# Sparse layer's norms by column sums and a selection moved ahead; the first section with late loads

## The reference

```python
# start of the first block
mod = silu(c) @ w_ada + b_ada                    # six parts; the first two make shift and scale
h = rms_norm(x, g_mix) * (1 + scale) + shift
proj = h @ w_in                                  # latents q_lat (256), kv_lat (128), k_rope (32), ...

# sparse layer, the parts up to its attention
proj = rmsnorm(x) @ w_in                         # c_q (256), c_kv (128), k_idx (64), w_idx (8)
c_q, c_kv, k_idx = rmsnorm(c_q), rmsnorm(c_kv), rmsnorm(k_idx)
q_idx = einsum(c_q, w_q_idx)                     # 8 heads of 64
rel = relu(einsum('bqhd,bsd->bqhs', q_idx, k_idx))
score = einsum('bqh,bqhs->bqs', w_idx, rel)      # masked where the key is later than the query
sel = top_k(score, 128)                          # per query; attention goes over these keys alone
p = masked_softmax(q_abs . c_kv + bias)          # 8 heads
o = p . c_kv
```

## Time and profile before

| | |
|---|---|
| time of the kernel before, median of 3 runs | 2147.43 us (2146.58 to 2153.29) |
| the profiled execution's own time | 2157.64 us, span 2155.7 us |
| TensorE busy | 2009.7 us, 93% of the span |
| VectorE, ScalarE, GpSimd busy | 1005.3, 633.1, 156.7 us |
| granted TensorE clock, mean | 0.96 of full speed |

### The profile page before, as it was taken

How to read it: one execution, slowest core, us unless ns; L and a number is a source line. 1 busy time by engine, 2 the same in 40 slices (tenths; PEclk the granted TensorE clock), 3 DMA queues, 4 the chain that set the end, 5 groups by cost and what they waited for, 6 DMA issues and landing times.

```text
span 2155.7 us, 23513 instructions
## 1 busy us (share of the span) xinstructions
PE 2009.7 (93%) x8895; PEld 1347.8 (63%) x8895; DVE 1005.3 (47%) x1870; ACT 633.1 (29%) x1194; POOL 156.7 (7%) x169
## 2 busy tenths in 40 slices
PE   6989889995999996987999999999899999999998
PEld 3457666673333333535678888875555877888886
DVE  5255544334212115579465545552114757545554
ACT  3373621232111112244442222220024634222222
POOL 1000000020111112103010000020000001000001
PEclk9999999997999997897999999999998999999999
DMA  8323324355999776110122323231431012323211
GB/s 300 132 103 114 121 78 156 119 205 218 408 394 356 290 299 247 52 40 1 48 109 79 117 79 116 79 107 50 153 126 40 1 40 78 115 81 109 86 39 40
DMA packets 103605, 287.06 MB, mean 133 GB/s; under 512 B 13514, under 2 KB 24472, under 8 KB 90448
## 3 DMA queue, kind: packets, MB, share of 16 engines
q1 hardware_dynamic: 91360, 266.24, 33.3%
q0 software_dynamic: 10112, 16.81, 2.2%
q10 hardware_dynamic: 2032, 2.65, 0.4%
HBM read 329.64 MB, written 21.02 MB: 163 GB/s over the span
## 4 chain that ended last, share of the span: by engine, by line
PE 85%; DVE 6%; ACT 2%; DMA 2%; issue 2%; POOL 1%; ACTq 1%; SPq 0%; DVEq 0%; POOLq 0%
PE bank L1282 15%; PE bank L1284 14%; PE bank L1283 14%; PE bank L1199 12%; PE bank L1664 8%; PE bank L1690 4%; PE bank L1241 3%; PE bank L1253 2%; PE bank L1267 2%; PE bank L1850 1%; PE bank L1648 1%; PE bank L1485 1%; PE bank L1273 1%; POOL chunk_mask L1062 1%; DMA weight_ring<-in_w_ada 1%
## 5 line engine op out<-in xcount | busy, mean ns | idle before, releaser
L1284 PE MATMUL bank<-hidden_high,weights_low 128*128 128x512 f32 x896 | 352.1, 393 | 0.0
L1282 PE MATMUL bank<-hidden_high,weights_high 128*128 128x512 f32 x704 | 277.3, 394 | 11.5 <-DVE weights_low L2584 5.0
L2976 DVE TENSOR_TENSOR weights_low<-weight_ring,weights_high 128x1024 fp32r<-128x1024 f32 x128 | 161.1, 1259 | 269.2 <-ACT weights_high L2120 269.2
L1283 PE MATMUL bank<-hidden_low,weights_high 128*128 128x512 f32 x640 | 250.0, 391 | 0.0
L2120 ACT ACTIVATE weights_high<-weight_ring 128x1024 fp32r<-128x1024 f32 x128 | 135.7, 1060 | 323.5 <-PE bank L1284 323.5
L1282 PE MATMUL bank<-normed_high,weights_high 128*128 128x512 f32 x512 | 200.8, 392 | 4.1 <-DVE weights_low L2976 4.0
L1283 PE MATMUL bank<-normed_low,weights_high 128*128 128x512 f32 x512 | 199.9, 390 | 0.0
L1284 PE MATMUL bank<-normed_high,weights_low 128*128 128x512 f32 x512 | 199.8, 390 | 0.0
L1284 PEld LDWEIGHTS bank<-hidden_high,weights_low 128*128 128x128 f32 x896 | 170.4, 190 | 36.2
L1664 PE MATMUL bank<-weight_ring,arena 128*64 128x512 f32 x464 | 174.1, 605 | 4.5 <-issue 2.7
L1199 PE MATMUL bank<-arena,weight_ring 128*128 128x512 f32 x396 | 176.5, 601 | 0.0
(11 more groups left out here) (479 smaller groups left out, 3115.2 us busy)
## 6 DMA issues: line engine op xcount, KB each, us to landing
weight_ring<-in_w_up SPq DMA_DIRECT2D x16, 2048.0 KB, 8.4
weight_ring<-in_w_down SPq DMA_DIRECT2D x16, 2048.0 KB, 7.6
weight_ring<-in_w_gate SPq DMA_DIRECT2D x29, 1024.0 KB
weight_ring<-in_w_up SPq DMA_DIRECT2D x29, 1024.0 KB
weight_ring<-in_w_ada SPq DMA_DIRECT2D x12, 2048.0 KB, 12.7
weight_ring<-in_w_down SPq DMA_DIRECT2D x19, 1024.0 KB
hT<-in_w_down SPq DMA_DIRECT2D x19, 1024.0 KB
weight_ring<-in_w_in SPq DMA_DIRECT2D x7, 2048.0 KB, 12.6
```

The costliest lines, as they stand in the source:

```text
L1282: pe.matmul(dst, high, rhs_high, start=first, stop=False)
L1283: pe.matmul(dst, high, rhs_low, start=False, stop=False)
L1284: return pe.matmul(dst, low, rhs_high, start=False, stop=last)
L2976: dve.tensor_tensor(piece_half(w_lo, ch, q), piece_of(ch, q), piece_half(w_hi, ch, q).bitcast(F32), ALU.subtract).then_inc(s_wlo, 1)
```

## The change

It has these parts:

1. *First section.* 24 of ScalarE's 31 small loads move to SP: the vectors behind the first two `w_ada` chunks, the positions, rotation tables and router biases behind a new empty chunk (`"none"`) that waits for the ring's first slot. The latents' weights leave the ring for the arena, so all four `w_ada` chunks have a slot at once. x's squares are summed token-major by VectorE; root and reciprocal are of 128x4; the reciprocals are put on diagonals and spread by one matmul with ones. `MOD_PE` becomes 4, 4, 0, 0. The angles and sines move behind the first modulation. ScalarE's copies of the value tiles go to VectorE.
2. *Sparse projections.* The latents are scored without their roots. The squares of x and of the latents are summed by matmuls with 32 columns in four column groups side by side, then folded to a column per token and norm. Roots and reciprocals are of 128x20. The key's root comes back as a row (`k_row`), the query's as a column (`q_scale`), both applied when block's scores are copied. The latents for the attention and x itself are scaled later by spread rows; x in steps 19 to 26 of the attention. The index weights are summed in column groups too.
3. *Order.* The scores of block 3 come right behind those of block 2, ahead of `dq`; nine of block 3's sixteen rounds stand ahead of the attention, the other seven at every second step from step 0.
4. *Attention.* The probabilities are normalised by ScalarE instead of VectorE.
5. *GpSimd.* `add_squares(1)` is gone, so the bias table's load is issued right behind the last scatter; GpSimd makes two of the four diagonals.

```diff
-MOD_PE = (4, 3, 2, 2)
+MOD_PE = (4, 4, 0, 0)
+TOP_EARLY = 9
+X_NORMED_FROM = 19
...
     for c in MOD_FIRST:
         chunk(("ada", c), last=G[("mod_sum", c)])
-        if c == MOD_FIRST[1]:
-            chunk("in_lat", last=G["kr"])
+    chunk("none", 0, last=0)
...
                 put_ada(c)
                 if c == MOD_FIRST[1]:
-                    put("in_lat", [(0, kt(w_in, 0, 416))])
+                    load_vectors()
+                    sp.dma_start(w_lat, kt(w_in, 0, 416)).then_inc(s_latw, 16)
+            put("none", [])
+            sp.dma_start(sbuf_s[:, 0, :].bitcast(I32), bass.AP(a["positions"].tensor, 0, [[0, P], [1, T]]))\
...
+            for t in range(NT):
+                dve.wait_ge(s_x[t], 16)
+                junk = hT[:, 2 * t:2 * t + 2, :].rearrange("p a b -> p (a b)")
+                ins = dve.tensor_tensor_reduce(out=junk, in0=x_tok[:, t, :], in1=x_tok[:, t, :], scale=1.0, scalar=0.0,
+                                               op0=ALU.mult, op1=ALU.add, accum_out=x_root[:, t:t + 1])
...
-            add_squares(1)
             pool.wait_ge(mm_done, done(G[("moe_D", STEPS - 1)] + 1))
             pool.dma_start(toe[:, :, :], toe2_dram.rearrange("h p u -> p h u")).then_inc(s_toe, 16)
...
+            for half in range(2):
+                for c in range(4):
+                    last = pe.matmul(psum(g)[32 * c:32 * c + 32, :], w[:, 4 * half + c, 488:520],
+                                     hT[:, 4 * half + c, :], start=(half == 0), stop=(half == 1),
+                                     skip_group_check=True)
...
+            for j in range(KD):
+                pe.wait_ge(s_dxsq, j + 1)
+                pe.matmul(psum(g)[32 * (j % 4):32 * (j % 4) + 32, :], stat_sel[:, j, :], dx_sq[:, j, :], start=(j < 4),
+                          stop=False, skip_group_check=True)
...
             index_scores(1)
+            for n in range(2):
+                pe.wait_ge(s_ddiag, n + 1)
+                token_row(G["token_rows"] + n, n)
             index_scores(2)
+            for n in range(2):
+                pe.wait_ge(s_ddiag_p, n + 1)
+                token_row(G["token_rows_late"] + n, 2 + n)
+            index_scores(3)
+            pe.wait_ge(s_dn, 3)
...
+                    if 0 <= s - 1 < ITEMS:
+                        i = s - 1
+                        h, qt, n = dsa_shape(i)
+                        act.wait_ge(s_rcp, i + 1)
+                        act.activation(sbuf_p[:, i % 3, 0:n], sbuf_p[:, i % 3, 0:n], ACT.Copy,
+                                       scale=stat[:, i % 3, 2:3]).then_inc(s_norm, 1)
...
-                        dve.tensor_scalar(sbuf_p[:, i % 3, 0:n], sbuf_p[:, i % 3, 0:n], stat[:, i % 3, 2:3], None,
-                                          ALU.mult).then_inc(s_norm, 1)
...
+            g_read(dve, G["token_rows"])
             top_rounds(1, 0, TOPK // 8)
+            g_read(dve, G["token_rows"] + 1)
+            for m in range(2):
+                dve.tensor_tensor(cq_n[:, m, :], cq_n[:, m, :], cq_row, ALU.mult).then_inc(s_dn, 1)
+            g_read(dve, G["token_rows_late"])
+            dve.tensor_tensor(ckv_n[:, 0, :], ckv_n[:, 0, :], ckv_row, ALU.mult).then_inc(s_dn, 1)
             top_rounds(2, 0, TOPK // 8)
+            top_rounds(3, 0, TOP_EARLY)
...
-                if s < TOPK // 8:
-                    top_rounds(3, s, s + 1)
+                if s % 2 == 0 and TOP_EARLY + s // 2 < TOPK // 8:
+                    top_rounds(3, TOP_EARLY + s // 2, TOP_EARLY + s // 2 + 1)
+                if s == X_NORMED_FROM:
+                    g_read(dve, G["token_rows_late"] + 1)
+                if X_NORMED_FROM <= s < X_NORMED_FROM + KD:
+                    x_normed(s - X_NORMED_FROM)
```

More of the change, by code:

```diff
@@ L1454, in _, with bias_and_vectors @@
                         last.then_inc(mm_done, 1)
[L1455 to L1465, removed]
+            first_bias_table()
+            g = G["norm_mix"]
+            pe.wait_ge(s_xdiag, 1)
+            tile(g, psum(g)[:, :], [(ones[:, :], x_diag)]).then_inc(mm_done, 1)
+            def bias_and_vectors():
+                first_bias_reversed()
+                pe.wait_ge(s_vec, 16 * 13)
+                g = G["vec"]
+                pe.transpose(begin(g)[:, 0:VN], vec_in[0:VN, :], ident[0:VN, 0:VN]).then_inc(mm_done, 1)
             pe.wait_ge(s_cs, 1)
-            mod_row_sum(MOD_FIRST[0], 0, norm_mix)
+            mod_row_sum(MOD_FIRST[0], 0, bias_and_vectors)
             mod_row_sum(MOD_FIRST[1], 1)
@@ L2165, in _ @@
                            scale=CA_SCALE).then_inc(s_a, 1)
+            for j in range(1, KD, 2):
+                evac(G["tp_x"] + j, xT[:, j, :])
+            g = G["table_T"]
+            evac(g, table1_T[:, :], psum(g)[:, 0:3 * H])
             g = G["toe1"]
@@ L2221, in _ @@
             for m in range(3):
+                if m == 1:
+                    rope_tables()
                 act.wait_ge(mm_done, done(g + m))
@@ L2236, in _ @@
                 evac(g, k_mla[64:128, 2 * p + 1, :], psum(g)[64:128, :])
-            for t in range(NT):
-                evac(G["uv"] + t, v_mla[:, t, :])
             act.wait_ge(s_rv, 16)
@@ new lines, in _ @@
+            dve.wait_ge(s_xroot, 1)
+            link(dve.reciprocal(x_root[:, :], x_root[:, :]))
+            dve.wait_ge(mm_done, done(G["toe2"] + 1))
+            dve.tensor_tensor(x_diag.rearrange("p (t q) -> p t q", t=NT),
+                              ident[:, :].unsqueeze(1).broadcast_to([P, NT, P]),
+                              x_root[:, :].unsqueeze(2).broadcast_to([P, NT, P]), ALU.mult).then_inc(s_xdiag, 1)
+            for j in range(0, KD, 2):
+                evac(G["tp_x"] + j, xT[:, j, :])
@@ new lines, in _, with over_root, first_modulation @@
+            dve.wait_ge(s_cs, 1)
+            mod_partial(MOD_FIRST[0], 0, MOD_PE[0], KD)
+            def over_root(j0, j1):
+                for j in range(j0, j1):
+                    g_read(dve, G["tp_x"] + j)
+                    ins = dve.tensor_tensor(hT[:, j, :], xT[:, j, :], psum(G["norm_mix"])[:, :], ALU.mult)
+                    ins.then_inc(s_unit if j < KD - 1 else freed[G["norm_mix"] % BANKS], 1)
+            def first_modulation(half):
+                for c in MOD_FIRST[2 * half:2 * half + 2]:
+                    mod_add(c)
+                    g_read(dve, G[("mod", c)])
+                scale_of(scale1, 1, "g_mix", half).then_inc(s_mod1, 1)
@@ new lines, in _ @@
+            dve.wait_ge(mm_done, done(G["norm_mix"]))
+            over_root(0, 4)
+            g = G["vec"]
+            evac(g, vecT[:, 0:VN], psum(g)[:, 0:VN])
+            g_read(dve, g)
+            dve.tensor_tensor(gain_sq[:, :], g_first[:, :], g_first[:, :], ALU.mult).then_inc(s_gain, 1)
+            dve.tensor_tensor(gain_both[:, :], g_first[:, :], col("g_attn_2", 0, KD), ALU.mult).then_inc(s_gain, 1)
+            dve.wait_ge(s_gain, 2)
+            mod_partial(MOD_FIRST[1], 1, MOD_PE[1], KD)
@@ L2726, in _ @@
                     .then_inc(freed[g % BANKS], 1)
+            for t in range(NT):
+                evac(G["uv"] + t, v_mla[:, t, :])
             pair_attention("mla")
```

432 lines of the change are left out of this document (200 added, 232 removed).

## The result

The changed kernel takes 2129.74 us (median of 4, 2126.02 to 2132.34) against 2149.31 (4, 2146.58 to 2153.29) beside it: a ratio of 0.9906, 95% interval 0.9881 to 0.9931, or 19.6 us less. The forecast was 41.9 less. A few executions on record took far longer than their neighbours (2163, 3332, 7080 and 11072 us); the ratios leave them out.

The account below looks back on a forecast made before the run. TensorE holds 85% of the chain of waits, while VectorE paces attention steps 0 to 15. The terms -14.4 + 3.1 - 14.0 - 16.6 = -41.9, off the median 2147.43, give 2105.5 us, range 2093 to 2122.

Parts of the forecast that it names:

- the term of 14.0 for projections and selection: Sparse layer, first projection to VectorE's first attention score: 108.1 us against 122.1 now, 14.0 less.
- the first scores last 9.1 as now: Sparse layer, block 1's scores behind the projections: they keep their length of 9.1 us.
- What follows is the same up to the experts' end: From first attention through the experts: unchanged, so the first section's 14.4 us earlier start is kept whole.
- the 0 behind the attention: Stretch from the output weights to the end: the forecast sum has no term for it.
- First section: Start to first attention: latents' halves at 34.8 and 52.8 us, attention starting 14.4 earlier.
- rivals 1 and 4: Late small vector loads: 1 loses half the first section's gain, 2113, chance 0.13; 4 serves them singly, 2171, chance 0.03.
- The hand-over's 3.1: Experts to sparse layer: the bias table's 2 MB load, now behind the last scatter, adds 3.1 us to the path.
- The two groups of tiny matmuls were priced at 1.8: Sparse projections: these matmuls take 1.8 us, an unseen shape, with bounds 0.5 to 4.
- VectorE's chain: Sparse layer, selection rounds of blocks 1 to 3 with latents by their rows: 56.2 us in sum.
- Attention: Attention loop: steps 0 to 15 take 24.5 us against 39.1, 14.6 less; steps 16 to 31 2 less net.
- Rival 2: TensorE stays at 1.2 GHz through attention steps 8 to 15, steps 0 to 15 take 29, table load costs 6: 2113, chance 0.15.
- the 1.5 to 2 set down for that: Attention steps 19 to 26: VectorE's eight scalings of x collide with GpSimd's additions, 1.5 to 2 us lost.

## Why the prediction was wrong, by its own steps

The direction came true, and half of the gain: 18.8 to 20.9 us of 41.9. The step that failed is the term of 14.0 for projections and selection, which measured about 2 to 3; in it "the first scores last 9.1 as now" is what broke. "What follows is the same up to the experts' end" and the 0 behind the attention failed too, by smaller amounts.

The stretches, in us, both profiles of each kernel; the change is between their means:

```
stretch                              before          after          change   forecast
start to first attention             110.5, 110.1    97.2, 96.7     -13.4    -14.4
first attention to first projection  728.0, 722.8    734.7, 734.6   + 9.3    + 3.1
first projection to attention score  122.1, 117.6    118.0, 117.2   - 2.3    -14.0
attention score to output weights     89.7,  88.9     73.1,  73.9   -15.8    -16.6
from there to the end               1105.4, 1105.5  1107.6, 1109.9  + 3.3      0
```

**First section: right.** Latents at 34.55 and 53.78 (forecast 34.8, 52.8), first attention at 97.15 (96.1). The 1 us missing is there when the second half starts. That half then takes 13.52 us for the same 24 matmuls that took 12.07, at the lower clock for part of it, yet from its start to the first attention it is 43.4 us, as forecast (43.3). The vectors were turned at 25.29 (needed at 26), so rivals 1 and 4 are out.

**"What follows is the same up to the experts' end": wrong by some 4 us.** The hand-over's 3.1 is right (3.3 in the trace, 4 when removed). The rest is given back in mixer and experts: from the first attention to the last scatter it is 705.4 and 701.4 us in the two profiles of before, and 705.0 to 710.1, 707.9 on average, in the ten of versions with the new first section, whatever their sparse part. Part of it shows: VectorE waits longer for a block's modulation weights, 6.83 against 5.42 in the first profile of before, and TensorE then waits 1.51 where it had none:

```profile
180.78 0.49 DVE L2639 TENSOR_SCALAR arena<-weight_ring,silu_c 128x512 f32<-128x512 f32 x1 [6.83 <-DMA weight_ring<-in_w_ada]
```

The load is issued 13.3 us earlier, as all else, and lands 9.1 us later instead of 7.7 (8.2 in the second profile of before). The second run of the changed kernel has 6.78 for this wait. Why the load lands later is open; the stretch differs by 5.2 between two executions of one kernel, so its exact share can't be read. The first section alone is worth 11.2 by its times, so by them 2.2 of the 13.4 are given back.

**Projections and selection: the step that failed.** The prediction's sum for the changed kernel was 108.1; it took 118.0. "The first scores last 9.1 as now": they lasted 15.5, since the clock fell, and with VectorE's start behind them this is 7.4 of the 9.9 (18.1 from first score to VectorE's first operation, against 10.7). The two groups of tiny matmuls were priced at 1.8 and took that; what was left out is what they do to the clock of narrow work behind them. Another 1.3 is in the projections (42.5 against 41.2) and 1.2 in VectorE's chain (57.4 against 56.2). The experiments show the cause: a wide query between gives 53.6 instead of 59.8 to 60.6 from first projection to VectorE's start. The other side of this term was one draw: the way of before took 122.1, 117.6 and, in the kernel with the first section alone, 122.2 us. The two long ones are of executions above their kernels' medians (2157.64 over 2147.43, 2148.32 over 2140.97), the short one of an execution below its own (2146.82 under 2151.83). So part of the 14.0, up to 4.5 us, may not have been there to win in a median execution.

**Attention: right.** 23.1 for steps 0 to 15 (forecast 24.5), 1.2 less behind them (forecast 2). The forecast's 39.1 for before is the length of two windows, which begin 0.6 ahead of the first score; from score to score it is 38.6. Rival 2, TensorE at 1.2 GHz through steps 8 to 15, did not come. The scalings of x took 0.73 each (one 0.77), so VectorE lost nothing to GpSimd's additions there; the 1.5 to 2 set down for that did not come there.

**Behind the attention: 1 to 5 lost, forecast 0.** The stretch takes 1105.4 and 1105.5 us before and 1105.5 with the first section alone. Of the nine profiles with the new sparse layer five have 1106.3 to 1106.7, the changed kernel 1107.6, and three 1109.9 to 1110.2; these three have a mean clock of 0.91 from 1500 to 1700 us where the others have 0.94 or 0.95, and one of them is the changed kernel itself, so no edit explains it. One us is a wait: TensorE waits longer for the compression's weights, before and after (line, releaser, us in total, times, longest):

```profile
PE bank L1869 <- DMA weight_ring<-in_cmp_w_v: 0.7, 1, 0.7
```

```profile
PE bank L1933 <- DMA weight_ring<-in_cmp_w_v: 1.8, 1, 1.8
```

**The base.** The terms were read from an execution 10.2 us above the median and taken off the median whole. Part of that excess was in the terms, as the ways of 122.1 and 117.6 show; and the neighbouring series of the kernel before had medians of 2149.3 to 2152.9, not 2147.4.

## What to carry to other kernels

Short matmuls can cost more than their own time: here 1.8 us of them, with narrow matmuls right behind, brought 6 to 7 us at the lower clock. Read the granted clock behind such groups, and try one wide group of independent work between. Here this costs nothing, and gave 6 to 7 us of 2130 in the traces; in the kernel before, where the tiny group itself lasts 9.99 us, wide work behind it came too late. A term that is a difference of two long stretches needs two profiles of before: between them the same stretch moved by 4.5 us, a third of the gain forecast for it. And when an engine starts a loop late because it works ahead for it, look at how much of the work fits in that loop's idle time.

## What the runs showed of the hardware

TensorE's clock can fall with no idle time in its records. In the kernel before it falls inside the 64 matmuls of 8 columns, in a window where TensorE is busy 12.00 of 12.00 us (876 to 888, mean clock 0.75). In the changed kernel it falls about 3 us behind the first tiny matmul, with 0.13 us idle at 875.5; the orders with a query between have the same 0.13 us and no fall. What in these stretches brings the clock down no run shows.

The collision of VectorE and GpSimd falls on the one that starts second. At 977.02 the scaling of x starts, two SBUF inputs, and takes 0.73; GpSimd's addition starts at 977.11 and takes 1.50 where it took 1.01 alone. All eight scalings are like this: GpSimd's four additions of 384 beside them take 1.50 or 1.51, the four of 512 take 1.72 to 1.78 instead of 1.27.

```profile
974.94 1.01 POOL L1208 TENSOR_TENSOR small<-toeplitz_bias,arena 128x384 f32<-128x384 f32 x1 [0.32 <-DVE stat L2552]
977.11 1.50 POOL L1208 TENSOR_TENSOR rtmp<-toeplitz_bias,arena 128x384 f32<-128x384 f32 x1 [1.16 <-DVE stat L2552]
```

The other way round, GpSimd's product started at 881.82, and VectorE's operation on 128x4 elements behind it took 1.85, where such ones took 0.15 to 0.16 at 875 us. Those at 875 also had a product of GpSimd beside them (873.98, 2.92 us), but at most one of their inputs was in SBUF:

```profile
882.32 1.85 DVE L3119 SCALAR_TENSOR_TENSOR index_scale<-latent_rstds 128x4 f32<-128x4 f32 x1
```

The Trainium skill's page "SBUF — State Buffer", section "Who interferes with whom", says that the order of issue and not the shape of the operation decides who blocks. The trace agrees, by these rows; the prediction had put the price on VectorE alone.
